# z projection spread over the value pass and the prompt attention of a one-core decoder step

## The chip, the cores and the metric

One Trainium2 chip, one core. The metric is the device time of the whole program in microseconds (us), as the median of three runs.

## What is computed

One inference step of a two-layer decoder trunk, all in float32, for a prompt of 512 positions and for 8 sequences of 4 new positions each that have 2048 past positions in a paged cache. Width 2048, 8 heads, two query/key halves of 128 per head, values of 256 per head.

```python
# layer 1: short gated convolution
b_gate, c_gate, hx, z = jnp.split(rms_norm(x, norm_g) @ w_in, 4, axis=-1)
x = x + (b_gate * conv3_causal(c_gate * hx) * silu(z)) @ w_out
# shared keys and values
k, v = jnp.split(rms_norm(x, norm_kv) @ w_kv, [QK_DIM], axis=-1)      # k: norm, rotary
# layer 2: differential attention
q, z = jnp.split(rms_norm(x, norm_g) @ w_in, [QK_DIM], axis=-1)        # q: norm, rotary
w = softmax(q1 k1 * scale) - lam * softmax(q2 k2 * scale)              # per head, masked
x = x + (rms_norm(w @ v, subln_g) * (1 - lam_init) * silu(z)) @ w_out
```

The keys and values of the past (two times 134 MB) are gathered page by page through a page table of 8 times 16 pages of 128 positions.

## The kernel before, in words

Six stages follow each other, each a block of its own with a barrier behind it: read the inputs, the convolution layer's input projection, its output projection, `project_and_score`, `attention`, `project_out`. The change touches the fourth and the fifth. Activations are held with the features on the partitions; 544 columns stand for 512 prompt positions and 32 new ones. A float32 projection is made of three products of fp32r parts (high times high, low times high, high times low), so a block of 128 output columns takes 96 matmuls of 272 columns (L1032 and L1040 in the fourth stage). Its weights are loaded in pairs of blocks (2 MB, `load_pair`), scaled by the norm gain on ScalarE (L834), copied to the high part by ScalarE (`split_hi`, L848), and the low part is the difference, made by VectorE (`split_lo`, L947).

**The fourth stage, `project_and_score`**, has 64 steps, one block each: 16 of q, 16 of z, 16 of k, 16 of v. VectorE evacuates block n-1 in step n and finishes block n-2: q and k are normed and rotated (L979 to L986), z becomes a SiLU gate with a reciprocal of 3.55 us (L971 to L974). q, k and z of the prompt go to scratch in DRAM; k and v are also turned on TensorE and written out as rows. Between this work lies the **key pass**: scores of the new positions against the past keys, cut into 128 units. A unit turns a quarter of a page's columns for four pages on VectorE (`turn_unit`, L996, four 32x32 block transposes of 128x512) and multiplies them with the queries on TensorE (`score`, L1081, 16 float32 matmuls, which are 32 records). Two units, an even and an odd one, share the four pages. A constant says how many units lie in each step, and their letters A to D say where in the step VectorE and TensorE do them. In VectorE's step n the order is: evacuate(n-1), A, finish(n-2), split_lo(n+1), B, C, D.

Half pages of keys (512 KB) arrive in a ring of six. The load of page n waits until the odd unit has turned page n-6:

```python
sp.wait_ge(kt_ready, (2 * (before // GRP) + 1) * GRP + before % GRP + 1)
```

**The fifth stage, `attention`**, begins with the softmax of the first sequence and then has 8 slots. Slot r is the value product of sequence r over its 16 pages (L1533, pages of 1 MB in a ring of eight) and, between the pages, the prompt attention of head r in four query blocks, with the softmax of sequence r+1 in five steps on VectorE. TensorE's order in a slot is written out: prompt scores of block 0, then pages 0 to 15 with turns, scores and sums behind given pages, the product with the prompt's values behind page 13 (L1504), the new values, and the sum of squares of the head's output (L1512). ScalarE issues the loads of the next head's q, k and v at the start of the next slot, when the previous head's output is done (`load_inner`), and of its z when the previous gate is done (`load_gate`). GpSimd multiplies the head's output by its norm and by the gate and writes it to scratch.

The prediction follows the lines named here, and L958 and L956 (evacuations), L1048 (sum of squares of a block), L1285 (copy of turned prompt weights), L1430 (copy of a head's output), L1489 (prompt scores).

## Time and profile before

| | |
|---|---|
| median of 3 runs | 2751.94 us (2750.53 to 2756.54) |
| profiled execution, its own time | 2754.07 us |
| its span, first to last instruction | 2752.3 us |
| TensorE / VectorE / ScalarE / GpSimd busy | 2481.1 / 1494.2 / 1017.1 / 346.9 us |
| mean granted TensorE clock | 0.956 of 2.4 GHz |
| moved by DMA | 512.01 MB, mean 186 GB/s |
| fourth stage, first to last matmul of its blocks | 1033 to 2057 us of the span |
| fifth stage, first to last value matmul | 2091 to 2506 us of the span |

Busy time is the union of an engine's instructions; a matmul's duration is its latency, several overlap, so the distance of two starts in the timeline is what an instruction costs TensorE. The granted clock is a share of 2.4 GHz; 0.5 is its lower level, 1.2 GHz.

### The profile page before, as it was taken

The page shows a single profiled execution, that of the slowest core. Times are in us where ns is not written, and L with a number is a line of the kernel's source. Part 1 is how long each engine was busy: PE and PEld are TensorE (multiplying, and loading weights), DVE is VectorE, ACT ScalarE, POOL GpSimd, SP SyncE. Part 2 cuts the span into 40 slices and gives each one's busy share as a digit, 9 for nine tenths or more (in the row PEclk, how much of TensorE's full clock was granted, in tenths as well). Part 3 has the DMA queues.
Part 4 walks back from the last instruction along what each step waited for, and adds up shares of the span by engine and source line. Part 5 has one row for each costly group of instructions (what it writes and reads, how often), then busy time and mean ns, then how long its engine had stood idle before and what let it go on. Part 6 is the DMA issues. An engine that isn't in the chain of part 4 may idle for free. (4 is left out here: it accounts for less than half of the span.)

```text
span 2752.3 us, 52718 instructions
## 1 busy us (share of the span) xinstructions
PE 2481.1 (90%) x21599; PEld 2229.3 (81%) x21599; DVE 1494.2 (54%) x1926; ACT 1017.1 (37%) x1826; POOL 346.9 (13%) x142
## 2 busy tenths in 40 slices
PE   6999999999999999999999999989995556656998
PEld 5999999999999989999898999978882122213998
DVE  3565565666563343456888887766664334324221
ACT  4121111112112226776445687745541212224121
POOL 5233333233320110000000000000000110010000
PEclk9999999999999999999999999999997778877999
DMA  4323332323323323244766778778869989986343
GB/s 129 92 77 92 92 92 76 92 83 85 92 76 112 112 86 99 85 153 135 248 237 239 268 266 267 266 243 267 281 231 361 385 343 374 381 363 245 113 120 87
DMA packets 387584, 512.01 MB, mean 186 GB/s; under 512 B 12618, under 2 KB 319700, under 8 KB 370964
## 3 DMA queue, kind: packets, MB, share of 16 engines
q1 hardware_dynamic: 328436, 449.67, 48.1%
q10 hardware_dynamic: 57792, 55.74, 5.8%
q0 software_dynamic: 1200, 4.46, 0.4%
q8 instruction: 106, 1.74, 0.3%
...
## 5 line engine op out<-in xcount | busy, mean ns | idle before, releaser
L1032 PE MATMUL psum<-x_hi,w_hi 128*128 128x272 f32 x2048 | 434.2, 293 | 3.0 <-PEq L503 3.0
L106 PE MATMUL psum<-x_hi,w_hi 128*128 128x272 f32 x2048 | 427.0, 289 | 8.4 <-DVEq L413 8.4
L106 PE MATMUL psum<-x_lo,w_hi 128*128 128x272 f32 x2048 | 426.2, 289 | 0.0
L1032 PE MATMUL psum<-x_lo,w_hi 128*128 128x272 f32 x2048 | 426.0, 289 | 0.0
L996 DVE STREAM_TRANSPOSE h_keys_turned<-h_ring 128x512 f32<-128x512 f32 x512 | 325.1, 682 | 144.3 <-DMA h_ring<-in_cache_k_dram 140.6
L1032 PEld LDWEIGHTS psum<-x_hi,w_hi 128*128 128x128 f32 x2048 | 321.7, 190 | 18.8 <-issue 18.8
L106 PEld LDWEIGHTS psum<-x_hi,w_hi 128*128 128x128 f32 x2048 | 321.5, 189 | 9.5 <-ACTq L405 9.1
L1032 PEld LDWEIGHTS psum<-x_lo,w_hi 128*128 128x128 f32 x2048 | 322.4, 189 | 0.0
L106 PEld LDWEIGHTS psum<-x_lo,w_hi 128*128 128x128 f32 x2048 | 320.9, 188 | 0.0
L366 POOL TENSOR_TENSOR w_raw<-w_raw,params 128x2048 f32<-128x2048 f32 x63 | 245.9, 3903 | 509.6 <-DMA w_raw<-in_w_in_a_dram 502.7
L1040 PE MATMUL psum<-x_hi,w_lo 128*128 128x272 f32 x2048 | 287.1, 296 | 0.0
L1040 PEld LDWEIGHTS psum<-x_hi,w_lo 128*128 128x128 f32 x2048 | 267.0, 190 | 9.4 <-issue 5.9
L114 PE MATMUL psum<-x_hi,w_lo 128*128 128x272 f32 x2048 | 266.4, 287 | 0.0
L114 PEld LDWEIGHTS psum<-x_hi,w_lo 128*128 128x128 f32 x2048 | 260.2, 188 | 0.0
L834 ACT ACTIVATE w_raw<-w_raw,params 128x256 f32<-128x256 f32 x496 | 201.6, 495 | 103.9 <-DMA w_raw<-in_w_kv_dram 58.6
L385 ACT ACTIVATE w_hi<-w_raw 128x2048 fp32r<-128x2048 f32 x64 | 122.4, 1912 | 305.1 <-PE psum L114 280.4
L422 DVE TENSOR_TENSOR w_lo<-w_raw,w_hi 128x2048 fp32r<-128x2048 f32 x64 | 175.5, 2742 | 104.1 <-ACT w_hi L385 104.1
L947 DVE TENSOR_TENSOR w_lo<-w_raw,w_hi 128x2048 fp32r<-128x2048 f32 x63 | 143.6, 2280 | 54.6 <-ACT w_hi L848 54.6
L1081 PE MATMUL psum<-h_keys_turned,h_q_blocks 128*32 128x128 f32 x4096 | 141.2, 280 | 35.1 <-DVE h_keys_turned L996 34.9
L1489 PE MATMUL psum<-head 128*128 128x128 f32 (+3 forms) x128 | 49.3, 518 | 126.4 <-DMA head<-out_new_v_prompt_dram 125.7
L1533 PE MATMUL psum<-ring,weights 128*8 128x512 f32 x1024 | 146.0, 671 | 8.0 <-DMA ring<-in_cache_v_dram 8.0
L1081 PEld LDWEIGHTS psum<-h_keys_turned,h_q_blocks 128*32 128x32 f32 x4096 | 106.4, 111 | 55.8 <-DVE h_keys_turned L996 29.3
...
## 6 DMA issues: line engine op xcount, KB each, us to landing
h_ring<-in_cache_k_dram SPq DMA_DIRECT2D x256, 512.0 KB, 6.1
ring<-in_cache_v_dram SPq DMA_DIRECT2D x128, 1024.0 KB, 12.5
...
```

The lines of the kernel that those rows point to most:

```text
L106: pe.matmul(out[:, g, 0:GT], m.WH[s][:, k * P:(k + 1) * P], x[:, k * T + g * GT:k * T + (g + 1) * GT], start=(k == 0 and x is xh), stop=Fa ...
L114: last = pe.matmul(out[:, g, 0:GT], m.WL[s][:, k * P:(k + 1) * P], xh[:, k * T + g * GT:k * T + (g + 1) * GT], start=False, stop=(k == KT ...
L366: pool.tensor_tensor(tiles(raw[p % 2][:, :]), tiles(raw[p % 2][:, :]), m.PAR[:, GA:GA + KT].unsqueeze(2).to_broadcast([P, KT, P]), ALU.mul ...
L385: act.activation(m.WH[p % 2][:, :], raw[p % 2][:, :], ACT.Copy).then_inc(hi_ready, 1)
L422: dve.tensor_tensor(m.WL[p % 2][:, :], raw[p % 2][:, :], m.WH[p % 2][:, :].bitcast(F32), ALU.subtract).then_inc(lo_ready, 1)
L834: ins = act.activation(wk, wk, ACT.Copy, scale=m.PAR[:, gain + k:gain + k + 1])
L947: dve.tensor_tensor(columns(m.PAIR_LO, n), src, tiles(m.WH[n % 2][:, :].bitcast(F32)), ALU.subtract).then_inc(lo_ready, 1)
L996: dve.transpose(kth[u % 2][:, s * QUAD:(s + 1) * QUAD], ring[n % NRING][:, u % 2 * QUAD:(u % 2 + 1) * QUAD]).then_inc(kt_ready, 1)
L1032: pe.matmul(psum[n % 2][:, g, 0:GT], m.WH[n % 2][:, k * P:(k + 1) * P], x[:, k * T + g * GT:k * T + (g + 1) * GT], start=(k == 0 and x is ...
L1040: last = pe.matmul(psum[n % 2][:, g, 0:GT], w[:, k, :], m.XH[:, k * T + g * GT:k * T + (g + 1) * GT], start=False, stop=(k == KT - 1), ski ...
L1081: last = pe.matmul(bank[a * TURN:(a + 1) * TURN, u // 2 % 2, :, u % 2, :], qblk[half % 2][:, ch * TURN:(ch + 1) * TURN], keys[:, :, a * 4 ...
L1533: last = pe.matmul(out[c * B:c * B + 2 * NEW, :], wt[r % 2][:, weights_at(p, c):weights_at(p, c) + 2 * NEW], ring[(r * NPG + p) % NR][:, c ...
```

## The change

The z blocks leave the fourth stage, which becomes 48 steps (q, k, v). The 128 key units go to steps 17 to 47, four or five in a step, with a letter E behind D. VectorE turns two pages with one instruction and lets go of ring pages in pairs; the turned keys have three buffers where there were two; a query block has 16 columns where it had 32; the rows to be written have one buffer where there were two. The first z pair is loaded, scaled and split at the end of the fourth stage.

The fifth stage projects the 16 z blocks: blocks 0 and 1 ahead of the first slot, blocks 2r+2 and 2r+3 in slot r (0 to 6), 14 matmuls ahead of each of the pages 0 to 6 and 8 to 14. Their evacuation, gate and low part are put on VectorE, their scaling, high part and exponential on ScalarE; the gates stay in SBUF, and the z scratch and its loads go. Values come as half pages (512 KB) in a ring of seven, scores of one sequence at a time, the new values in four parts. The next head's q and k are loaded when the last prompt scores are done, its v when its last product is done.

The diff, cut to its core:

```diff
-KINDS = "qzkv"
+KINDS = "qkv"
...
-FIRST_UNIT_STEP = KT + 2
-UNITS_IN_STEP = [2, 2, 2, 3] * 4 + [3, 3, 3, 2] * 4 + [4, 3, 4, 3, 3, 4, 3] * 2
+FIRST_UNIT_STEP = KT + 1
+UNITS_IN_STEP = [2] + [4, 4, 4, 4, 5] * 6
+NKTH = 3
+QN = P // TURN * NEW
...
-    return dict(zip({2: "AC", 3: "ACD", 4: "ABCD"}[many], range(first, first + many)))
+    return dict(zip({2: "CD", 4: "ABCD", 5: "ABCDE"}[many], range(first, first + many)))
...
-    unit = 8 * half + 9
+    unit = 8 * half + 10
...
-        ring = [sb(f"ring{s}", [P, HALF]) for s in range(NRING)]
-        kth = [sb(f"keys_turned{f}", [P, GRP * QUAD]) for f in range(2)]
-        qblk = [sb(f"q_blocks{f}", [P, HALF]) for f in range(2)]
+        ring = sb("ring", [P, NRING * HALF])
+        kth = [sb(f"keys_turned{f}", [P, GRP * QUAD]) for f in range(NKTH)]
+        qblk = [sb(f"q_blocks{f}", [P, HALF // TURN * QN]) for f in range(2)]
...
-                    sp.wait_ge(kt_ready, (2 * (before // GRP) + 1) * GRP + before % GRP + 1)
+                    sp.wait_ge(kt_ready, (2 * (before // GRP) + 1) * 2 + before % GRP // 2 + 1)
...
-                    after(act, rows_out[s], rows_in_slot(n) * 32)
-                    act.activation(rows[s][:, :], m.PS[:, ROWS, :], ACT.Copy).then_inc(rows_ready, 1)
-                    act.activation(srows[s][:, :], m.PS[0:GS, SROWS, 0:G * P], ACT.Copy).then_inc(rows_ready, 1)
+                    after(act, rows_out, turns_before(n) * 32)
...
-                after(dve, unit_scored, u - 1)
-                for s in range(GRP):
-                    n = u // 2 * GRP + s
+                after(dve, unit_scored, u + 1 - NKTH)
+                for pair in range(GRP // 2):
+                    n = u // 2 * GRP + 2 * pair
                     if u % 2 == 0:
-                        dve.wait_ge(page_in[n % NRING], 16 * (n // NRING + 1))
-                    dve.transpose(kth[u % 2][:, s * QUAD:(s + 1) * QUAD],
-                                  ring[n % NRING][:, u % 2 * QUAD:(u % 2 + 1) * QUAD]).then_inc(kt_ready, 1)
-                if u % 4 == 1 and u >= 5:
+                        for x in (n, n + 1):
+                            dve.wait_ge(page_in[x % NRING], 16 * (x // NRING + 1))
+                    dve.transpose(kth[u % NKTH][:, pair * 2 * QUAD:(pair + 1) * 2 * QUAD].rearrange("p (s x) -> p s x", s=2),
+                                  ring[:, n % NRING * HALF:(n % NRING + 2) * HALF].rearrange("p (s x) -> p s x", s=2)
+                                  [:, :, u % 2 * QUAD:(u % 2 + 1) * QUAD]).then_inc(kt_ready, 1)
+                if u % 4 == 2 and u >= 6:
...
-                        last = pe.matmul(bank[a * TURN:(a + 1) * TURN, u // 2 % 2, :, u % 2, :],
-                                         qblk[half % 2][:, ch * TURN:(ch + 1) * TURN], keys[:, :, a * 4 + c, :],
+                        last = pe.matmul(bank[a * TURN:a * TURN + QN, u // 2 % 2, :, u % 2, :],
+                                         qblk[half % 2][:, ch * QN:(ch + 1) * QN], keys[:, :, a * 4 + c, :],
...
-                hi_part(n, first)
+                hi_part(n, range(5))
                 if "D" in before:
                     score(before["D"])
-                hi_part(n, second)
+                hi_part(n, range(5, 11))
+                if "E" in before:
+                    score(before["E"])
+                hi_part(n, range(11, KT))
...
-    NR = 8
+    NR = 7
...
+            w, col0, _ = head_weights(d, "z")
+            def load_pair(p):
+                after(sp, zdone, 2 * p - 2)
+                sp.sem_inc(granted, 1)
+                sp.dma_start(tiles(m.PAIR_RAW[p % 2]), w.rearrange("(k p) n -> p k n", p=P)
+                             [:, :, col0 + 2 * p * P:col0 + 2 * (p + 1) * P]).then_inc(pair_in[p % 2], 16)
...
+                for f in range(2):
+                    n = 2 * (i * NPG + p) + f
+                    if n >= NR:
+                        sp.wait_ge(v_used, (n - NR) // 2 + 1)
+                    sp.sem_inc(granted, 1)
+                    sp.dma_start(ring[:, n % NR * HALF:(n % NR + 1) * HALF], cache_v[ds(page, 1), :, f * HALF:(f + 1) * HALF]
+                                 .rearrange("o p n -> (o p) n")).then_inc(half_in[n % NR], 16)
...
+            load_pair(1)
             sp.wait_ge(ids_in, 16)
             for i in range(NSEQ):
                 for p in range(NPG):
-                    n = i * NPG + p
-                    if n >= NR:
-                        sp.wait_ge(v_used, n - NR + 1)
-                    load(cache_v, i, p, n % NR)
+                    load_values(i, p)
+                    if p == 3 and i + 2 < NZ // 2:
+                        load_pair(i + 2)
...
+            def load_probs(i):
+                after(act, wt_ready, i)
+                act.dma_start(pr[:, :], st.SCORES[i]).then_inc(probs_in, 16)
...
+            def load_qk(r):
+                after(act, prompt_scored, r * TT)
...
+            def split_hi(b):
+                if not 1 <= b < NZ:
+                    return
+                after(act, zdone, b - 1)
+                after(act, zscaled, 2 * (b // 2))
+                act.activation(tiles(m.WH[b % 2][:, :]), zcolumns(m.PAIR_RAW, b), ACT.Copy).then_inc(zhi, 1)
+            def scale_half(p, f):
+                if not 1 <= p < NZ // 2:
+                    return
+                if f == 0:
+                    act.wait_ge(pair_in[p % 2], 16 * ((p + 1) // 2))
+                wp = m.PAIR_RAW[p % 2]
+                for k in range(f * KT // 2, (f + 1) * KT // 2):
+                    wk = wp[:, k * 2 * P:(k + 1) * 2 * P]
+                    ins = act.activation(wk, wk, ACT.Copy, scale=m.PAR[:, GB + k:GB + k + 1])
+                ins.then_inc(zscaled, 1)
...
             def slot(r):
-                if r:
-                    load_inner(r)
-                load_gate(r)
+                gate_exp(2 * r + 1)
                 prompt_exps(r, 0)
                 prompt_weights(r, 0)
+                split_hi(2 * r + 3)
                 prompt_exps(r, 1)
                 prompt_weights(r, 1)
+                scale_half(r + 2, 0)
                 prompt_exps(r, 2)
                 if r + 1 < NSEQ:
                     softmax_exp(r + 1)
                 prompt_weights(r, 2)
+                gate_exp(2 * r + 2)
                 prompt_exps(r, 3)
+                if r + 1 < H:
+                    load_qk(r + 1)
                 prompt_weights(r, 3)
+                scale_half(r + 2, 1)
+                split_hi(2 * r + 4)
                 act.wait_ge(o_taken, r + 1)
+                if r + 1 < H:
+                    load_v(r + 1)
                 act.activation(pp, o, ACT.Square).then_inc(osq_ready, 1)
                 act.wait_ge(osq_sum, r + 1)
-                rsqrt(act, o_ln, r * 2, m.PS[:, PSC, :], VD, m, ro[:, :])
+                rsqrt(act, o_ln, r * 2, m.PS[:, PSC, :], VD, m, ro)
+                if r + 1 < NSEQ:
+                    group_new_weights(r + 1)
+                if r + 2 < NSEQ:
+                    load_probs(r + 2)
                 take_rows(r)
...
+            def finish(b):
+                if b >= NZ:
+                    return
+                t = ztile[b % 4]
+                dve.wait_ge(zexp, b + 1)
+                chain_z.link(dve.tensor_scalar(zr[:, :], zr[:, :], 1.0, None, ALU.add))
+                chain_z.link(dve.reciprocal(zr[:, :], zr[:, :]))
+                chain_z.link(dve.scalar_tensor_tensor(out=t[:, :], in0=t[:, :], scalar=m.GSUB[:, b % 2:b % 2 + 1],
+                                                      in1=zr[:, :], op0=ALU.mult, op1=ALU.mult))
+                dve.tensor_copy(st.ZS[:, b * NT:(b + 1) * NT].rearrange("p (g t) -> p g t", g=G),
+                                grouped(t[:, :])[:, :, GP:GT]).then_inc(zready, 1)
...
+                evacuate(2 * r + 1)
+                prompt_max(r, 0, prompt)
                 step(0)
-                prompt_max(r, 0, prompt)
                 prompt_mix(r, 0, prompt)
+                finish(2 * r + 1)
+                prompt_max(r, 1, prompt)
                 step(1)
-                prompt_max(r, 1, prompt)
                 if r:
                     take_out(r - 1)
                 prompt_mix(r, 1, prompt)
+                split_lo(2 * r + 3)
                 step(2)
                 prompt_max(r, 2, prompt)
                 prompt_mix(r, 2, prompt)
+                evacuate(2 * r + 2)
                 prompt_max(r, 3, prompt)
                 step(3)
+                finish(2 * r + 2)
                 prompt_mix(r, 3, prompt)
+                split_lo(2 * r + 4)
                 step(4)
...
+            soft_max(0, first_soft)
+            split_lo(1)
+            soft_diag(0, first_soft)
+            evacuate(0)
+            soft_shift(0, first_soft)
+            soft_den(0, first_soft)
+            soft_weights(0, first_soft)
+            finish(0)
+            split_lo(2)
...
+            def project(b, part):
+                for at in range(part[0], part[1]):
+                    if at == 0:
+                        after(pe, zhi, b)
+                        after(pe, zevac, b)
+                    if at == 64:
+                        after(pe, zlo, b)
+                    if at < 64:
+                        k, x, g = at // 4, (m.XH, m.XL)[at // 2 % 2], at % 2
+                        w = m.WH[b % 2][:, k * P:(k + 1) * P]
+                    else:
+                        k, x, g = (at - 64) // 2, m.XH, at % 2
+                        w = zcolumns(m.PAIR_LO, b)[:, k, :]
+                    last = pe.matmul(zout[:, g, 0:GT], w, x[:, k * T + g * GT:k * T + (g + 1) * GT], start=(at < 2),
+                                     stop=(at >= 94), skip_group_check=True)
+                if part[1] == 96:
+                    last.then_inc(zdone, 1)
...
+            def project_in(r, p):
+                if 2 * r + 2 < NZ and p % 8 < 7:
+                    b, at = 2 * r + 2 + p // 8, p % 8 * 14
+                    project(b, (at, min(at + 14, 96)))
             def slot(r):
                 nxt = r + 1 < NSEQ
-                out = m.PS[:, OUT[r % 2], :]
+                out = m.PS[:, OUT, :]
                 prompt_scores(r, 0)
                 pe.wait_ge(wt_ready, r + 1)
-                after(pe, osb_ready, r - 1)
                 for p in range(NPG):
+                    project_in(r, p)
+                    if p == 0:
+                        after(pe, osb_ready, r)
                     value_in(pe, r, p)
...
             score_new()
-            pe.wait_ge(dve_tail, 1)
+            project(0, (0, 64))
             pe.wait_ge(new_masked, 1)
             turn_max(0)
+            project(0, (64, 96))
             spread_max(0)
+            project(1, (0, 32))
             sum_probs(0)
+            project(1, (32, 96))
+            pe.wait_ge(dve_tail, 1)
```

## Rows read from the trace of the kernel before

**Rows 1.** Busy time by stretch: window, length, engines with counts, granted clock, DMA share, GB/s.
```profile
1520.00:1765.00 245.00, 243.04 (x2797) 226.25 (x2795) 198.61 (x298) 188.21 (x385) 0.00 (x0) 1.00 0.79 263
...
1765.00:2060.00 295.00, 273.79 (x3378) 253.16 (x3370) 192.91 (x274) 147.61 (x374) 0.00 (x0) 0.98 0.78 262
...
2091.00:2507.00 416.00, 272.55 (x1533) 92.16 (x1533) 155.50 (x358) 96.62 (x218) 37.95 (x21) 0.81 0.91 368
```

**Rows 2.** Groups by form, whole span: high part of a block, z gate's reciprocal.
```profile
L848 ACT ACTIVATE w_hi<-w_raw 128x2048 fp32r<-128x2048 f32 x63 | 119.9, 1904 | 49.9 <-PE psum L1040 49.4
...
L972 DVE RECIPROCAL h_r<-h_r 128x544 f32<-128x544 f32 x16 | 56.8, 3553 | 0.6
```

**Rows 3.** TensorE in order of time, one k step: start, length, instructions, idle before.
```profile
1697.37 0.52 PE L1032 MATMUL psum<-x_hi,w_hi 128*128 128x272 f32 x2
...
1706.79 1.08 PE L1081 MATMUL psum<-h_keys_turned,h_q_blocks 128*32 128x128 f32 x32
...
1707.80 1.19 PE L1048 MATMUL psum<-h_r,ones 128*128 128x272 f32 x4
...
1714.61 0.52 PE L1032 MATMUL psum<-x_hi,w_hi 128*128 128x272 f32 x2
```

**Rows 4.** VectorE in order of time, the same k step.
```profile
1704.38 0.74 DVE L979 SCALAR_TENSOR_TENSOR h_tile<-h_plain,params,h_r 128x544 f32<-128x544 f32 x1
...
1708.43 2.28 DVE L947 TENSOR_TENSOR w_lo<-w_raw,w_hi 128x2048 fp32r<-128x2048 f32 x1
...
1710.63 2.48 DVE L996 STREAM_TRANSPOSE h_keys_turned<-h_ring 128x512 f32<-128x512 f32 x4
...
1718.05 0.71 DVE L996 STREAM_TRANSPOSE h_keys_turned<-h_ring 128x512 f32<-128x512 f32 x1 [0.95 <-DMA h_ring<-in_cache_k_dram]
```

**Rows 5.** Turns of keys (L996) alone: window, length, VectorE busy and count.
```profile
1810.00:2060.00 250.00, 122.21 (x192) 0.99 0.81 271
```

**Rows 6.** VectorE groups from 1765 to 2060 us.
```profile
L996 DVE STREAM_TRANSPOSE h_keys_turned<-h_ring 128x512 f32<-128x512 f32 x214 | 136.2, 683 | 80.7 <-DMA h_ring<-in_cache_k_dram 77.3 <-PE psum L1081 3.2
...
L956 DVE TENSOR_TENSOR h_tile<-psum,rs 128x544 f32<-128x544 f32 x16 | 11.1, 695 | 15.3 <-DMA k_scratch<-h_tile 12.8 <-PE psum L1040 2.6
```

**Rows 7.** VectorE evacuates block 17, in order of time.
```profile
1273.78 0.72 DVE L958 TENSOR_TENSOR h_plain<-psum,rs 128x544 f32<-128x544 f32 x1 [2.29 <-PE psum L1040]
```

**Rows 8.** TensorE from the last blocks to the first value page.
```profile
2057.44 1.95 PE L1081 MATMUL psum<-h_keys_turned,h_q_blocks 128*32 128x128 f32 x64
...
2066.76 1.08 PE L1062 MATMUL psum<-ident,h_tile 128*128 128x128 f32 x4 [6.56 <-ACT h_srows L860]
...
2073.24 1.89 PE L1463 MATMUL psum<-q_sample,k_sample 128*32 128x32 f32 x32 [4.97 <-PEq L1756]
...
2090.91 5.10 PE L1533 MATMUL psum<-ring,weights 128*8 128x512 f32 x24
```

**Rows 9.** TensorE in slot 2, and its last value pages.
```profile
2210.34 1.19 PE L1489 MATMUL psum<-head 128*128 128x128 f32 x4 [15.09 <-DMA head<-out_new_v_prompt_dram]
...
2240.74 1.90 PE L1533 MATMUL psum<-ring,weights 128*8 128x512 f32 x16
...
2243.43 1.98 PE L1512 MATMUL psum<-head,ones 128*128 128x512 f32 x4
...
2504.17 1.90 PE L1533 MATMUL psum<-ring,weights 128*8 128x512 f32 x16
```

**Rows 10.** ScalarE scales a pair of blocks, in order of time.
```profile
1714.89 6.51 ACT L834 ACTIVATE w_raw<-w_raw,params 128x256 f32<-128x256 f32 x16 [3.19 <-DMA w_raw<-in_w_kv_dram]
```

**Rows 11.** ScalarE in slot 2: exponentials of query block 2.
```profile
2224.91 0.58 ACT L1280 ACTIVATE head<-psum,prompt_max 128x384 f32<-128x384 f32 x1
```

**Rows 12.** VectorE in slot 2: end of its mix, start and end of the softmax weights.
```profile
2226.89 0.62 DVE L1393 SCALAR_TENSOR_TENSOR head<-head,prompt_inv 128x384 f32<-128x384 f32 x1
...
2233.41 0.55 DVE L1360 RECIPROCAL inv_denom<-psum 128x64 f32<-128x64 f32 x1
...
2235.84 0.67 DVE L1370 TENSOR_TENSOR weights<-probs 128x512 f32<-128x512 f32 x1
```

307 lines of the change are left out of this document (166 added, 141 removed).

## Prediction

> **What bounds the kernel now.** I read the busy time by stretch first. TensorE is busy 243.0 of 245 us while k blocks and keys run together, 273.8 of 295 us with v blocks and keys, but only 272.6 of 416 us in the value pass, at a granted clock of 0.81 [rows 1]. The reader is to see one engine with holes in one stage alone. There the DMA share is 0.91. So the change has something to fill: 16 blocks of projection are taken out of a stage that TensorE fills and put into one that it doesn't. The question is what bounds the shorter fourth stage once TensorE no longer does, and how much of the value pass's holes survive.
>
> **Part 1, the fourth stage.** On TensorE a high part of 64 matmuls with one unit between them takes 9.42 us, from 1697.37 to 1706.79; a unit takes 1.01, so a matmul costs 0.13 us with the seams and a block of 96 about 12.1 [rows 3]. Removing 16 blocks takes 16 x 12.1 = 193 us from TensorE. A k step with three units takes 17.24 us (1697.37 to 1714.61); with 4.2 units it would take 17.24 + 1.2 x 1.1 = 18.6, a v step, without the sum of squares (0.9), 17.7. If TensorE set the pace, steps 18 to 47 (16 that finish q or k, 14 that don't) would take 16 x 18.6 + 14 x 17.7 = 545 us.
>
> I think that VectorE and the ring of key pages set it. VectorE turns a unit in four times 0.6 = 2.4 us; finishing a k block takes 4.05 (1704.38 to 1708.43), the low part 2.2 [rows 4]. With 4.2 units, evacuation and the turned scores a k step has 17.5 us of VectorE work against TensorE's 18.6, without any wait. The waits come from the ring: page n may be loaded only when page n-6 has been turned by the odd unit, and the even unit needs it six pages later. When the odd unit begins at 1710.63, its second page is done at 1711.85; the page that takes this slot is turned at 1718.05: 6.2 us [rows 4]. Before, three units in a step left other work to cover this. At 5.2 us per unit (192 turns, so 48 units, in 250 us) [rows 5] it already shows: VectorE waited 77.3 us for pages in 295 us [rows 6].
>
> In the changed code pages are let go in pairs, so the second page's load is issued one issue later: I take 6.2 + 0.6 = 6.8 us. A cycle of two units (one group of four pages) is then 6.8, plus the even unit's second half and the odd unit's first half, 1.2 each: 9.2 us. VectorE work that lies between an even and an odd unit is added to it; what lies between an odd and an even one is hidden. By the written order, four units in a step and alternating phases, exposed are: in a v step low part 2.2 and turned scores 0.6 in one phase, evacuation 0.6 and turned scores 0.6 in the other, mean 2.0, or 1.0 per group; in a k step 6.9 in the one and 2.9 in the other, 2.3 per group. For pages behind a pair of weights, which are later, I add 0.2. So 10.4 us per group in v steps and 11.7 in k steps. Units 2 to 127 are 33.5 groups in k steps and 29.5 in v steps: 33.5 x 11.7 + 29.5 x 10.4 = 392 + 307 = 699 us. The first v evacuations wait for the scratch stores as before, 12.8 us [rows 6], of which the pages that land meanwhile give back more than half: 5 us.
>
> The start: block 17 is evacuated at 1273.78 [rows 7], and step 17 now has two units too, so step 18 begins at 1275. The last block ends at 1275 + 704 = 1979 us, before at 2057.4. From there to the first product of the fifth stage it was 15.8 us (2057.44 to 2073.24) [rows 8]; with one buffer for rows the last three stores follow one another, 5 us more. The fifth stage begins at 2000, **73 us earlier**. Bounds: TensorE's pace of 545 us (another 154 earlier) and the cycle with 7.8 us of latency (63 later).
>
> The query blocks of 16 columns, three key buffers and the new places of D and E cost and give nothing here, since TensorE waits for VectorE; their range is 0 to the rival below. ScalarE keeps some 17 us of work in a k step of 24; that covers it, and if it didn't, the steps would lengthen by the difference to 24, which is none.
>
> **Part 2, the start of the fifth stage.** Before, 17.7 us lie between its first product (2073.24) and the first value page (2090.91) [rows 8]. Now 192 matmuls precede it, 24.0 us, and 2 more while the clock is low. They fill the waits of the softmax (some 10 us); then come the gate and the low part of block 2 on VectorE before block 1 is evacuated, which block 2 waits for. Walking the order I get 36.6 us: **18.9 later**. Bounds 12 and 26.
>
> **Part 3, a slot.** Slot 2 takes 33.1 us from its scores to the sum of squares (2210.34 to 2243.43) [rows 9]; 1.4 of it is a wait for VectorE and about 2 the low clock after 15.09 us without work. Both go: 29.7. Added: 192 matmuls, 24.0 + 0.3. The sum of squares and the norm up to the next scores: 2.8. Together 56.8 us. The head wait of 15 us is gone, since q and k are asked for some 20 us and v some 50 us ahead of use.
> New waits, from the written orders:
> - Block 2r+3 begins at page 8 and needs block 2r+2 evacuated. VectorE does this behind the mix of query block 2, whose exponentials stand on ScalarE behind `scale_half`: 8 instructions, half of 6.51, 3.3 us [rows 10]. That starts when the turn behind page 6 is copied. Scaling 3.3, exponentials to end of mix 2.6 (2224.91 to 2227.51) [rows 11, 12], evacuation 0.7, hand-overs 0.5: 7.1, of which one page covers 0.9. With 0.5 for the copy: **6.7**.
> - At the end `split_hi` follows the second `scale_half` (3.3 + 1.9 [rows 2]), then on VectorE the low part 2.2, softmax weights 3.1 (2233.41 to 2236.51) [rows 12] and the copy of the output; page 14 with its matmuls, page 15 and the new values cover most of it: **2.7** remain.
> - Page 0 waits for ScalarE to copy the previous rows, behind four new copies and a load: **1.0**.
> Queues: on SP the z pair stands behind page 3 of a slot and waits for block 2r+1, which is done by then; pages 4 and 5 come after its 2 MB, some 7 us of DMA, and TensorE asks for page 4 some 12 us later, so I give it 0. On GpSimd's queue four small loads of the new values take the place of one, ahead of the first slot, at 0 for they are used at its end. The scores of one sequence (0.5 MB) are asked for at the end of a slot and used at the start of the one after.
> The gates' 2 x 5.1 us of VectorE (reciprocal 3.55 [rows 2]) lie beside TensorE's matmuls; without that cover they would come in front of max or mix, 5 us each.
> A slot is 67.2 us. DMA moves 16.8 + 1.6 + 2.1 + 1.0 = 21.5 MB in it, 320 GB/s, below the 368 of [rows 1], so it isn't the bound. From first to last value page: 7 x 67.2 + 34 for slot 7, which projects nothing = 504; before 2505.9 - 2090.9 = 415 [rows 8, 9]. **89 later.** Bounds for a slot: 60 (only half of each wait and 56.8 of work) and 71.
>
> **Sum** against the profiled span of 2752.3: -73 + 19 + 89 = +35, so 2787. The profiled execution took 2754.07, 2.1 above the median of 2751.94; against the median it is 2787 again, +1.3%.
>
> Clock: after 6.56 us without work four turns took 1.08 us [rows 8], at 1.2 GHz, where the clock had been full. A wait of 6.7 us in each slot could do the same to the next 3 us of projection, 1.5 us per slot. By the Trainium skill, "TensorE: Matmul & The Clock Gate", section "Loop structure matters more than you think", idle stretches between bursts bring the lower clock back; that speaks against this change, and with it the sum would be 2797. I leave it out because the later wait for VectorE absorbs most of it.
>
> **Rivals.**
> - *The page latency is mostly hidden* (0.17). TensorE sets the pace of the fourth stage: -227 + 108 = -119, 2633. For it: TensorE was busy 243 of 245 us in the k steps [rows 1]. Against: units came at 5.2 us, not 4.2, in the v steps [rows 5]. In this case the unit's cost counts. The Trainium skill, the same page, section "LDWEIGHTS (loading the stationary operand)", has a load's time go by its columns; 16 for 32 would save up to 50 us by it and give 2585. The records that bear on it start every 0.03 us [rows 3], which doesn't tell load from product.
> - *In between* (0.23): a latency near 6 us and slots of 63. The stage takes 45 us less, the slots 30 less: 2712. The sign turns at a latency of 6.2 with my slots, or slots of 62 with my latency.
> - *My forecast, slower* (0.48), own range 2750 to 2830: the ring of six pages decides, from 10.0 us per group on.
> - *The value pass becomes worse* (0.12): half pages and a lookahead of 3.5 pages instead of eight let DMA run dry whenever TensorE is held up; slots of 72: 2821.
> That the change doesn't do what it says could be so of the early head loads: if z weights and values go ahead of them, v is late at page 13. I give it nothing of its own.
>
> **How the numbers follow.** Predicted 2787. The range of 2645 to 2832 leaves out most of the first rival and the ends. About 0.2%, 5.5 us, is what a measurement can tell from no change. Faster 0.38 (both first rivals less their upper ends, and the low end of mine), same 0.07, slower 0.55.
>
> **What would show it.** Right: L996 waits for DMA by 250 us or more; k steps of 24 and v steps of 22 us; matmuls of the fourth stage with 5 us of waits for L996 in a step; slots of 67 us with one wait of 6 to 7 us at page 8 that VectorE's evacuation ends; no wait for head loads. Wrong: steps below 20 us, or slots that DMA ends.

## The result and the profile after

The changed kernel takes 2870.62 us (median of 4 runs, 2865.84 to 2878.27) against 2753.48 for the kernel before, a ratio of **1.0428, 95% interval 1.0401 to 1.0455**. The profiled execution took 2869.0 us with a span of 2867.2, 114.9 above the 2752.3 of before. I had predicted +35: the direction is right, the time is 39 us above the upper end of the range.

Where the 80 us between +35 and +115 lie is read from TensorE's timeline at the seams of the stages. The first product of the fifth stage (L1600) starts at 2028.96, predicted 2000: 29 us. From it to the first value page (2063.97) it is 35.0, predicted 36.6. From there to the first product with the new values, which follows the last value page (L1700 at 2620.35; L1554 at 2505.89 before), it is 556.4, predicted 504: 52.4 us. The three differences make the 80. So both stages that the change touches are worse than I had them, the slots more so.

The busy time by stretch, of the changed kernel (stretch, its length, then busy us of each engine with its instructions, the granted clock, DMA share, GB/s); the first three answer to [rows 1], the fourth is slots 0 to 6, from the scores of one to the scores of the last:

```profile
1520.00:1765.00 245.00, 192.45 (x2264) 170.80 (x2263) 147.42 (x151) 127.12 (x311) 0.00 (x0) 0.90 0.72 239
1765.00:2004.00 239.00, 202.23 (x2489) 182.61 (x2488) 138.76 (x121) 103.93 (x272) 0.00 (x0) 0.92 0.76 257
2064.00:2507.00 443.00, 371.64 (x2295) 233.68 (x2294) 224.91 (x346) 142.03 (x301) 28.39 (x20) 0.89 0.81 288
...
2059.00:2571.00 512.00, 434.69 (x2701) 273.85 (x2700) 265.73 (x411) 159.89 (x341) 34.04 (x24) 0.90 0.81 286
```

The reader is to see that TensorE, which filled 243 of 245 us of the k steps before, now has 192 there and a granted clock of 0.90; and that the value pass, whose holes were to be filled, has 371.6 of 443 busy, at 0.89, with DMA at 0.81, lower than before. No engine is full in any of these stretches. What holds the kernel are waits.

Of the same profile, the costliest groups (line, engine, what it does, count, busy us and mean ns, then the idle time before them and what ended it); the first answers to L996 of the kernel before, whose line for the whole span stands below:

```profile
L979 DVE STREAM_TRANSPOSE h_keys_turned<-h_ring 128x1024 f32<-128x1024 f32 x256 | 303.0, 1219 | 272.2 <-DMA h_ring<-in_cache_k_dram 272.2
...
L1068 PE MATMUL psum<-h_keys_turned,h_q_blocks 128*16 128x128 f32 x4096 | 155.6, 299 | 141.5 <-DVE h_keys_turned L979 138.5
...
L1679 PE MATMUL psum<-ring,weights 128*8 128x512 f32 x1024 | 143.4, 641 | 30.5 <-DMA ring<-in_cache_v_dram 27.7
L1592 PE MATMUL psum<-x_hi,w_hi 128*128 128x272 f32 x512 | 123.0, 325 | 41.0 <-DVE z_tile L1421 41.0
```

The same turns in the kernel before:

```profile
L996 DVE STREAM_TRANSPOSE h_keys_turned<-h_ring 128x512 f32<-128x512 f32 x512 | 325.1, 682 | 144.3 <-DMA h_ring<-in_cache_k_dram 140.6 <-PE psum L1081 3.4
```

VectorE waits 272 us for key pages, 141 before (the 77.3 of [rows 6] are those of 295 us of the stage), and TensorE 138.5 us for turned keys behind it, 34.9 before.

**One cycle of the ring**, VectorE's timeline in two k steps (start, length, line, xcount, in brackets the idle time before it and what ended it; `x3` from 1352.55 is the second half of an even unit and both halves of an odd one):

```profile
1352.55 3.50 DVE L979 STREAM_TRANSPOSE h_keys_turned<-h_ring 128x1024 f32<-128x1024 f32 x3 [4.73 <-DMA h_ring<-in_cache_k_dram]
1355.97 0.68 DVE L948 TENSOR_TENSOR h_plain<-psum,rs 128x544 f32<-128x544 f32 x1
1356.85 1.25 DVE L979 STREAM_TRANSPOSE h_keys_turned<-h_ring 128x1024 f32<-128x1024 f32 x1 [0.19 <-DMA h_ring<-in_cache_k_dram]
1362.11 1.25 DVE L979 STREAM_TRANSPOSE h_keys_turned<-h_ring 128x1024 f32<-128x1024 f32 x1 [4.02 <-DMA h_ring<-in_cache_k_dram]
...
1370.14 3.49 DVE L979 STREAM_TRANSPOSE h_keys_turned<-h_ring 128x1024 f32<-128x1024 f32 x3
1377.94 3.50 DVE L979 STREAM_TRANSPOSE h_keys_turned<-h_ring 128x1024 f32<-128x1024 f32 x3 [4.30 <-DMA h_ring<-in_cache_k_dram]
1381.36 0.69 DVE L948 TENSOR_TENSOR h_plain<-psum,rs 128x544 f32<-128x544 f32 x1
```

The odd unit's first half ends at 1354.85 and lets two pages go; the even unit that needs their successors goes on at 1362.11, 7.3 us later. I worked this out for all 63 groups of four pages after the first: in 59 of them VectorE waited there, and the pages came on average **7.6 us** after the turn that freed their places (6.2 to 11.3, the long ones behind a pair of weights). The second load of a pair, the one that VectorE waits for, goes out on average 1.9 us after that turn, 1.15 us behind the first of the pair, and lands 5.6 us after its issue. The evacuations at 1355.97 and 1381.36 make a k step of 25.4 us; the mean is 26.3 us for the k steps 18 to 33 and 22.7 us for the v steps 34 to 47.

**A slot**, TensorE's timeline (waits of over 0.7 us in slot 3, one value page without a wait, and the start of slot 4):

```profile
2282.01 1.22 PE L1626 MATMUL psum<-head 128*128 128x128 f32 x4 [0.78 <-ACT prompt_weights L122]
2302.95 1.82 PE L1679 MATMUL psum<-ring,weights 128*8 128x512 f32 x8 [3.26 <-DMA ring<-in_cache_v_dram]
...
2307.79 1.04 PE L1679 MATMUL psum<-ring,weights 128*8 128x512 f32 x8
...
2320.03 0.79 PE L1592 MATMUL psum<-x_hi,w_hi 128*128 128x272 f32 x2 [5.89 <-DVE z_tile L1421]
2353.43 2.97 PE L1650 MATMUL psum<-prompt_probs,ones 128*128 128x512 f32 x4 [2.43 <-ACT prompt_probs L1378]
2357.17 1.22 PE L1626 MATMUL psum<-head 128*128 128x128 f32 x4 [0.78 <-ACT prompt_weights L122]
```

The scores of the slots start at 2059.0, 2130.8, 2206.2, 2282.0, 2357.2, 2431.3, 2507.0 and 2570.8: a slot takes **75.3 us** from slot 1 to slot 5, predicted 67.2. Slot 6, for which no further z pair is loaded or scaled, takes 63.8. Behind each of the three long waits the matmuls take longer: eight with a value page 1.82 us where they take 1.04 without a wait, the first pair of the projection 0.79 where it takes 0.49 in the run with scaling later, the sums of squares 2.97 where they take 1.98 there. The wait at page 8 comes from ScalarE, as predicted:

```profile
2313.20 0.38 ACT L1319 ACTIVATE prompt_weights<-psum 128x256 f32<-128x256 f32 x1 [12.23 <-PE psum L1634]
2313.49 3.29 ACT L1345 ACTIVATE w_raw<-w_raw,params 128x256 f32<-128x256 f32 x8
2316.67 0.56 ACT L1312 ACTIVATE prompt_probs<-psum,prompt_max 128x384 f32<-128x384 f32 x1
```

What ends page 4 is in SP's queue: the load of the z pair (L1212) goes out 6 us into the slot, and the pages issued behind it are those for which TensorE waits until 2302.95. The pair lands 12.3 us after its issue, the two halves of page 4 13.6 and 14.9 us after it, and TensorE is ready for them 11.7 us after it. In slots 1 to 5 the pair takes 11.1 to 12.6 us and the second half of page 4 is there 13.9 to 15.2 us after the pair's issue, TensorE after 11.7 each time.

```profile
2274.42 13.44 SPq L1222 DMA_DIRECT2D ring<-in_cache_v_dram  x5
2287.97 0.39 SPq L1212 DMA_DIRECT2D w_raw<-in_w_in_b_dram  x1
2289.53 9.89 SPq L1222 DMA_DIRECT2D ring<-in_cache_v_dram  x7
```

### The profile page after: what moved, and what is told of

Read it like the earlier page. It is cut to its first block and busy times, and to the rows that moved or that the text cites. A ratio compares the mean times of both kernels' runs of the same rounds, so it can differ in the third digit from the quotient of the medians.

```text
span 2867.2 us, 53321 instructions
## 1 busy us (share of the span) xinstructions
PE 2553.8 (89%) x21599; PEld 2281.3 (80%) x21599; DVE 1488.0 (52%) x1671; ACT 1021.6 (36%) x1858; POOL 351.0 (12%) x152
## 5 line engine op out<-in xcount | busy, mean ns | idle before, releaser
L979 DVE STREAM_TRANSPOSE h_keys_turned<-h_ring 128x1024 f32<-128x1024 f32 x256 | 303.0, 1219 | 272.2 <-DMA h_ring<-in_cache_k_dram 272.2
L106 PE MATMUL psum<-x_hi,w_hi 128*128 128x272 f32 x2048 | 427.0, 289 | 8.4 <-DVEq L413 8.4
L106 PE MATMUL psum<-x_lo,w_hi 128*128 128x272 f32 x2048 | 426.0, 289 | 0.0
L1017 PE MATMUL psum<-x_hi,w_hi 128*128 128x272 f32 x1536 | 332.9, 298 | 3.0 <-PEq L503 3.0
L1017 PE MATMUL psum<-x_lo,w_hi 128*128 128x272 f32 x1536 | 324.6, 293 | 0.0
L106 PEld LDWEIGHTS psum<-x_lo,w_hi 128*128 128x128 f32 x2048 | 320.8, 188 | 0.0
L1068 PE MATMUL psum<-h_keys_turned,h_q_blocks 128*16 128x128 f32 x4096 | 155.6, 299 | 141.5 <-DVE h_keys_turned L979 138.5
L114 PE MATMUL psum<-x_hi,w_lo 128*128 128x272 f32 x2048 | 266.4, 287 | 0.0
L114 PEld LDWEIGHTS psum<-x_hi,w_lo 128*128 128x128 f32 x2048 | 260.1, 188 | 0.0
L1017 PEld LDWEIGHTS psum<-x_lo,w_hi 128*128 128x128 f32 x1536 | 246.9, 193 | 0.0
L1068 PEld LDWEIGHTS psum<-h_keys_turned,h_q_blocks 128*16 128x16 f32 x4096 | 110.9, 103 | 169.1 <-DVE h_keys_turned L979 90.0
L1025 PE MATMUL psum<-x_hi,w_lo 128*128 128x272 f32 x1536 | 227.9, 305 | 0.0
L422 DVE TENSOR_TENSOR w_lo<-w_raw,w_hi 128x2048 fp32r<-128x2048 f32 x64 | 173.0, 2703 | 104.2 <-ACT w_hi L385 104.2
L1025 PEld LDWEIGHTS psum<-x_hi,w_lo 128*128 128x128 f32 x1536 | 211.8, 200 | 7.4 <-issue 3.2
L830 ACT ACTIVATE w_raw<-w_raw,params 128x256 f32<-128x256 f32 x384 | 155.9, 494 | 98.3 <-DMA w_raw<-in_w_kv_dram 73.7
L1592 PE MATMUL psum<-x_hi,w_hi 128*128 128x272 f32 x512 | 123.0, 325 | 41.0 <-DVE z_tile L1421 41.0
## 6 DMA issues: line engine op xcount, KB each, us to landing
w_raw<-in_w_kv_dram SPq DMA_DIRECT2D x16, 2048.0 KB, 12.4
```

What stands on the lines that cost most here:

```text
L106: pe.matmul(out[:, g, 0:GT], m.WH[s][:, k * P:(k + 1) * P], x[:, k * T + g * GT:k * T + (g + 1) * GT], start=(k == 0 and x is xh), stop=Fa ...
L114: last = pe.matmul(out[:, g, 0:GT], m.WL[s][:, k * P:(k + 1) * P], xh[:, k * T + g * GT:k * T + (g + 1) * GT], start=False, stop=(k == KT ...
L422: dve.tensor_tensor(m.WL[p % 2][:, :], raw[p % 2][:, :], m.WH[p % 2][:, :].bitcast(F32), ALU.subtract).then_inc(lo_ready, 1)
L830: ins = act.activation(wk, wk, ACT.Copy, scale=m.PAR[:, gain + k:gain + k + 1])
L979: dve.transpose(kth[u % NKTH][:, pair * 2 * QUAD:(pair + 1) * 2 * QUAD].rearrange("p (s x) -> p s x", s=2), ring[:, n % NRING * HALF:(n % ...
L1017: pe.matmul(psum[n % 2][:, g, 0:GT], m.WH[n % 2][:, k * P:(k + 1) * P], x[:, k * T + g * GT:k * T + (g + 1) * GT], start=(k == 0 and x is ...
```

## The experiments

Theory: in the fourth stage the latency of a key page, on a ring of six, sets the pace; in the slots three waits, each of order and not of bandwidth, and the low clock behind them. Rivals: VectorE's written order holds TensorE in the fourth stage; DMA sets the slot.

### The fourth stage

**No key loads.** Only the first six pages are loaded; the scores are those of these pages.

```diff
                 if n >= NRING:
-                    before = n - NRING
-                    sp.wait_ge(kt_ready, ...)
+                    return
...
                         for x in (n, n + 1):
-                            dve.wait_ge(page_in[x % NRING], 16 * (x // NRING + 1))
+                            if x < NRING:
+                                dve.wait_ge(page_in[x], 16)
```

> The changed kernel with only the first six key pages loaded; all later turns work on the pages that are there, so no load of keys and no wait for one is left (the scores are those of six pages only). Theory (the ring's latency paces the fourth stage: 272 us of L979 waiting for pages, 734 us from step 17 to the end of block 47): TensorE's own work paces it, 545 us plus what VectorE's order adds, so the stage ends 150 to 190 us earlier and the whole takes 2680 to 2720 us; the granted clock of the stage is back near 1. Rival (VectorE's written order holds TensorE, and the page waits only fill time in which it would have been held anyway): the stage gets less than 60 us shorter, the whole stays above 2810 us. A TensorE wait for L979 of over 60 us would speak for the rival.

Measured: 2725.8 us in one run, 6 above the range of the theory and far below the rival's; the fifth stage begins at 1887.1, 142 us earlier, where the theory had 150 to 190. TensorE still waits 29.5 us for turned keys, which no page delays: so much of the stage is VectorE's order, and it is under the 60 us that would have spoken for the rival. From step 18 to the end of block 47 it takes 595 us where the changed kernel takes 729. The v steps take 17.2 us, with TensorE busy for 239 of 240 us; the k steps take 22.2 us, at a granted clock of 0.95, and all but 1 us of these waits lie there.

```profile
L979 DVE STREAM_TRANSPOSE h_keys_turned<-h_ring 128x1024 f32<-128x1024 f32 x256 | 297.6, 1212 | 18.3 <-PE psum L1068 18.1
...
L1068 PE MATMUL psum<-h_keys_turned,h_q_blocks 128*16 128x128 f32 x4096 | 139.6, 278 | 32.1 <-DVE h_keys_turned L979 29.5
```

**Pages let go one by one.**

```diff
-                for pair in range(GRP // 2):
-                    n = u // 2 * GRP + 2 * pair
+                for s in range(GRP):
+                    n = u // 2 * GRP + s
...
-    sp.wait_ge(kt_ready, (2 * (before // GRP) + 1) * 2 + before % GRP // 2 + 1)
+    sp.wait_ge(kt_ready, (2 * (before // GRP) + 1) * GRP + before % GRP + 1)
```

> The changed kernel, but each key page is turned and let go by itself, as in the kernel before (four turns of 0.6 us in a unit, not two of 1.2). In the changed kernel the page that VectorE waits for lands on average 7.6 us after the turn that frees its buffer, where I had taken 6.8. Theory (the two loads of a pair are issued together and share the DMA engines, which makes the later one late): latency falls to 6.2 to 6.8 us, some 0.9 us in each of 63 groups, 40 to 60 us less in the stage, the whole 2810 to 2835 us. Rival (the latency is that of one load, whoever lets it go, and of the weights in the queue): under 15 us of difference, 2855 to 2875 us.

Measured: 2824.6 us in one run, 46 less. Worked out as above from the timeline, the latency is now 6.4 us on average (112 waited pages), 1.2 less than in pairs. A load goes out 1.1 us after the turn that frees its place, where the second of a pair did after 1.9, and lands 5.2 us later, where that one took 5.6. So two thirds of the 1.2 are the second issue and one third is a slower landing; that the two loads of a pair share the DMA engines, as the theory has it, isn't shown, and could explain the landing alone. The gain came to the size that the theory gave. The waits of its turns:

```profile
L978 DVE STREAM_TRANSPOSE h_keys_turned<-h_ring 128x512 f32<-128x512 f32 x512 | 324.5, 682 | 200.0 <-DMA h_ring<-in_cache_k_dram 199.9
```

**Ring of eight.**

```diff
-NRING = 6
+NRING = 8
-NKTH = 3
+NKTH = 2
```

> The changed kernel with eight key pages in the ring in place of six, and two buffers of turned keys in place of three, which frees the room. A page is then asked for when the group before the last is turned, a whole group earlier. Theory (latency of the ring): a group of four pages takes about 8.8 us in place of 11.6, as TensorE's work sets it; the fourth stage ends 130 to 180 us earlier, the whole takes 2690 to 2740 us, below the kernel before. L979 waits for pages under 80 us. Rival (two buffers of turned keys are too few, or VectorE's order holds TensorE): the gain is under 60 us, the whole stays above 2810 us, and VectorE waits for units scored instead.

Measured: **2738.9 us (6 runs), ratio to the kernel before 0.9945, interval 0.9928 to 0.9962**: 132 us less than the changed kernel, and now 0.5% below the kernel before. The fifth stage begins at 1900.0, in place of 2029.0. Waits for pages fall from 272 to 62 us with a latency that is no shorter (median landing 6.6 us, 5.8 before); it is covered, since each page is asked for a group earlier.

```profile
L979 DVE STREAM_TRANSPOSE h_keys_turned<-h_ring 128x1024 f32<-128x1024 f32 x256 | 301.5, 1219 | 84.2 <-DMA h_ring<-in_cache_k_dram 62.0 <-PE psum L1068 21.9
...
h_ring<-in_cache_k_dram SPq DMA_DIRECT2D x256, 512.0 KB, 6.6
```

The rival falls: the order is unchanged, and there is one buffer of turned keys less. What it named is there, but small: VectorE now waits 21.9 us for TensorE's scores (L1068), as there are two buffers of turned keys, and TensorE 40.0 us for turned keys.

### The slots

**Scaling later**, alone on the changed kernel.

```diff
-                scale_half(r + 2, 0)
                 prompt_exps(r, 2)
                 if r + 1 < NSEQ:
                     softmax_exp(r + 1)
+                scale_half(r + 2, 0)
```

> The changed kernel, with the first half of the z pair's scaling (8 instructions, 3.3 us on ScalarE) moved behind the exponentials of query block 2 and of the sequence's softmax. Theory (this order delays the exponentials, the mix and the evacuation that block 2r+3 waits for, 5.89 us at page 8 in slots 0 to 5, and the clock is low after it): the wait falls below 2.8 us (what slot 6, without scaling, shows) and each of six slots gets 4 to 5 us shorter, the whole 25 to 30 us, 2840 to 2846 us. Rival (the DMA queue sets the slot, and time saved at page 8 comes back as waits for value pages): the slots stay at 75 us within 1 us, the whole 2864 to 2872 us, and waits for the ring grow by what page 8 loses.

Measured: 2849.9 us (ratio to before 1.0352, 1.0324 to 1.0380), 21 less. The slots 1 to 5 take 71.4 us, 3.8 less, of which the wait is 3.2 (5.89 to 2.71). Over seven slots it is 23 us; the fourth stage of this run ended 1.9 us later. That is short of the 25 to 30, at the size of 4 us per slot. The wait at page 4 grew by 0.2 us on average, so the time wasn't given back. The wait of 2.43 us at the sum of squares is unchanged, but in slots 0 to 2 the lower clock no longer follows it (1.98 us for four matmuls, 2.4 to 3.0 in the changed kernel); in slots 3 to 5 it does. So the length of a wait alone doesn't say whether it costs the clock. Slot 2's wait at page 8 and at its sum of squares:

```profile
2235.79 0.49 PE L1592 MATMUL psum<-x_hi,w_hi 128*128 128x272 f32 x2 [2.72 <-DVE z_tile L1421]
2269.17 1.98 PE L1650 MATMUL psum<-prompt_probs,ones 128*128 128x512 f32 x4 [2.43 <-ACT prompt_probs L1378]
```

**No value loads.** Only the first seven half pages are loaded; the attention over cached values is that of these.

```diff
                     if n >= NR:
-                        sp.wait_ge(v_used, (n - NR) // 2 + 1)
+                        return
...
-                eng.wait_ge(half_in[n % NR], 16 * (n // NR + 1))
+                if n < NR:
+                    eng.wait_ge(half_in[n % NR], 16 * (n // NR + 1))
```

> The changed kernel with only the first seven half pages of values loaded; all later pages use what is there, so that the only large load left in a slot is the z pair (the attention over the cached values is that of these half pages only). In the changed kernel a slot with a z pair takes 75.3 us from scores to scores, slot 6, which loads and scales no pair, 63.8, and slot 7, which projects nothing, some 50 where I had predicted 34. Theory (DMA ends page 4 in slots 1 to 5 by some 3.2 us each and sets slot 7): without the loads slots 1 to 5 lose 3 to 5 us each, slot 7 takes 33 to 37 us, the whole 2825 to 2840 us. Rival (the slot is set by the chain over ScalarE and VectorE, and the wait at page 4 only takes the place of another one): slots stay above 74 us and only slot 7 gets shorter, 2850 to 2858 us.

Measured: 2825.8 us in one run, 45 less. Slots 1 to 5 take 69.9 us, 5.4 less, and slot 7, from its scores to the last turn of rows, 40.2 in place of 55.7, which is above the 33 to 37 expected; from its first value page to the new values it takes 30.7 in place of 46.2. So DMA has 5 us in a slot and 15 in the last. The 69.9 us that remain are the slot's work, the two waits of order (5.89 and 2.43 us, both still there) and the low clock behind them.

**Ring of eight and a new order in the slot.**

```diff
                 if r + 1 < NSEQ:
                     softmax_exp(r + 1)
+                scale_half(r + 2, 0)
...
                     load_qk(r + 1)
+                scale_half(r + 2, 1)
                 prompt_weights(r, 3)
-                scale_half(r + 2, 1)
...
                 prompt_max(r, 2, prompt)
+                evacuate(2 * r + 2)
                 prompt_mix(r, 2, prompt)
-                evacuate(2 * r + 2)
```

> The ring of eight key pages, and in a slot: both halves of the z pair's scaling placed behind the exponentials of query blocks 2 and 3, and block 2r+2 evacuated before the mix of query block 2. Theory (each of the three waits in a slot is one of order, 5.9 us at page 8, 2.4 at the sum of squares, and the low clock after them): page 8 waits under 1 us, the sum of squares under 0.5, slots 0 to 5 take 66 to 69 us; with the ring's 2739 this gives 2680 to 2700 us. Rival (DMA sets the slot once TensorE is faster): the slots stay at 70 us or more, with ring waits of 5 us or more at page 4, 2705 to 2720 us.

Measured: 2668.2 us (0.9694, 0.9679 to 0.9708), 71 less than with the ring alone, where 39 to 59 were expected. The waits at page 8 and at the sum of squares are gone, a slot takes 64.4 us. The wait at page 4 is what is left, 2.8 to 4.1 us:

```profile
2118.45 0.71 PE L1626 MATMUL psum<-head 128*128 128x128 f32 x4 [0.78 <-ACT prompt_weights L122]
2138.78 1.89 PE L1679 MATMUL psum<-ring,weights 128*8 128x512 f32 x8 [3.53 <-DMA ring<-in_cache_v_dram]
2183.13 0.71 PE L1626 MATMUL psum<-head 128*128 128x128 f32 x4 [0.78 <-ACT prompt_weights L122]
```

**And the z pair in quarters** (behind value pages 2, 4, 6 and 8, with a semaphore for each half).

```diff
-                    if p == 3 and i + 2 < NZ // 2:
-                        load_pair(i + 2)
+                    if p in (2, 4, 6, 8) and i + 2 < NZ // 2:
+                        load_quarter(i + 2, p // 2 - 1)
```

> As the kernel with a ring of eight and the new order in the slot, with the z pair's load of 2 MB cut into four of 0.5 MB, put behind value pages 2, 4, 6 and 8 in the queue. Theory (the value pages behind the pair are late by its 2 MB, and the ring of 3.5 pages can't cover this): the wait at page 4, 3 us or more in slots 1 to 5, falls below 1 us, 15 to 25 us in all, 2660 to 2680 us. Rival (DMA bandwidth as a whole, not the order in the queue, sets it): the same waits in smaller pieces, under 5 us of difference to the run without quarters.

Measured: **2639.5 us (0.9593, 0.9579 to 0.9608)**, 29 less, where 15 to 25 were expected, and a slot of 59.2 us. The wait at page 4 is gone, and with it the lower clock behind it (1.89 us for eight matmuls in the lines above). The same bytes are moved in less time, at a DMA share of 0.95: it was the place of the pair in the queue, not the bandwidth. The pieces are smaller and most of them go out later; which of the two does how much, no run shows. The stretch of slots 0 to 6 (columns as above):

```profile
1926.00:2340.00 414.00, 398.22 (x2701) 248.05 (x2699) 251.73 (x411) 158.42 (x340) 33.78 (x24) 1.00 0.95 354
```

It has the 2701 matmuls of the 512 us in the changed kernel. Of the 98 us between them 36.5 are busy time (434.7 to 398.2), at a granted clock of 0.90 and of 1.00, and 61.5 are idle time.

**The mended slots with the ring of six** (order and quarters, `NRING = 6`, `NKTH = 3`).

> The changed kernel with the new order in the slot and the z pair in quarters, but with its own fourth stage: six key pages, let go in pairs, three buffers of turned keys. Theory (the two stages add up: the ring cost 132 us, order and quarters 100 us): 2765 to 2780 us, at or above the kernel before, so that the ring alone decides the sign. Rival (the gains overlap, for instance through the clock): outside 2755 to 2790 us.

Measured: 2773.7 us in one run. The two parts add up (2639.5 + 132), and without the ring's two pages even the mended slots don't make the change pay.

**Pages one by one in the ring of eight** (the edit of the single pages on top of the quarters).

> The kernel with ring of eight, new order and quarters (2639 us), and the key pages turned and let go one by one. Theory (with eight pages each is asked for a group earlier, so its latency of 6.4 or 7.6 us is covered either way; 40 us of TensorE waits for turned keys remain, at the two ends and behind weight pairs): 2628 to 2643 us. Rival (latency still paces a part of the stage): 2600 to 2625 us.

Measured: 2640.8 us (0.9592, 0.9576 to 0.9608), no difference. With each page asked for a group earlier, it costs nothing whether pages are let go in pairs or one by one; with the ring of six it cost 46 us.

### Parts of the change on the kernel before

**Early head loads.**

```diff
-                if r:
-                    load_inner(r)
                 load_gate(r)
...
                 prompt_exps(r, 3)
+                if r + 1 < H:
+                    after(act, prompt_scored, (r + 1) * TT)
+                    load_head(r + 1, 0)
+                    load_head(r + 1, 1)
                 prompt_weights(r, 3)
                 act.wait_ge(o_taken, r + 1)
+                if r + 1 < H:
+                    load_head(r + 1, 3)
```

> The kernel before with one part of the change alone: q and k of the next head are loaded behind the last scores of this one, v behind the last product with v, not all at the start of the slot; and TensorE waits for v at page 13 only. In the kernel before each of slots 1 to 7 begins with a wait for these loads, 15.09 us in slot 2. Theory (in that kernel the value pass is bound by DMA, share 0.91, 19.4 MB in a slot of 53 us, so the wait is time in which the ring fills up and is given back later): 0 to 25 us faster, and TensorE waits for value pages instead. Rival (the wait is on the path): 7 slots by 8 to 15 us, 55 to 100 us faster, 2650 to 2700 us.

Measured: 2704.2 us (0.9822, 0.9809 to 0.9836), 48 less: neither range. The value pass of the kernel before waits 123.7 us for heads in seven slots; 39% of that came out as time. Then DMA is full, at a slot of 46 us, and TensorE waits 42.3 us for pages in place of 8.0. The value pass, of the kernel before and of this one:

```profile
2091.00:2460.00 369.00, 241.97 (x1350) 81.66 (x1349) 143.34 (x325) 88.30 (x195) 32.53 (x18) 0.82 0.92 376
```

```profile
2091.00:2460.00 369.00, 284.97 (x1540) 92.77 (x1540) 157.85 (x365) 96.63 (x218) 38.15 (x21) 0.90 1.00 414
```

I had taken a share of 0.91 for full.

**Query blocks of 16 columns.**

```diff
-                        last = pe.matmul(bank[a * TURN:(a + 1) * TURN, u // 2 % 2, :, u % 2, :],
-                                         qblk[half % 2][:, ch * TURN:(ch + 1) * TURN], ...
+                        last = pe.matmul(bank[a * TURN:a * TURN + QN, u // 2 % 2, :, u % 2, :],
+                                         qblk[half % 2][:, ch * QN:(ch + 1) * QN], ...
```

> The kernel before with one part of the change alone: query blocks of 16 columns in place of 32 in the scores of the keys (4096 weight loads and matmuls in the fourth stage), with the banks blanked once. In the kernel before TensorE is busy 243 of 245 us of the k steps, so what a unit saves there is seen. Theory (a weight load of 16 columns takes as long as one of 32, in the traces 103 and 111 ns: no gain): within 0.2% of the kernel before. Rival (the load's time goes by its columns, as the Trainium skill's page on TensorE's matmul has it, in the section on the load of the stationary operand): 20 to 50 us faster, units of 0.7 us in place of 1.01.

Measured: 0.9992, interval 0.9981 to 1.0002 (12 runs). The weight loads of the fourth stage, 1270 to 2057 us, in the kernel before and in this one:

```profile
L1081 PEld LDWEIGHTS psum<-h_keys_turned,h_q_blocks 128*32 128x32 f32 x4032 | 104.7, 111 | 55.7 <-DVE h_keys_turned L996 29.3 <-issue 14.0
```

```profile
L1086 PEld LDWEIGHTS psum<-h_keys_turned,h_q_blocks 128*16 128x16 f32 x4032 | 100.9, 97 | 54.8 <-DVE h_keys_turned L998 27.5 <-issue 20.4
```

A unit of 32 records takes 1.07 us with 16 columns and 1.08 with 32 [rows 3]. The Trainium skill, "TensorE: Matmul & The Clock Gate", section "LDWEIGHTS (loading the stationary operand)", gives a load half the time for half the columns; here it went from 111 to 97 ns and none of it reached the time, so the measurement decides.

**The best that the study found with z left in place:** early heads, query blocks of 16, a ring of eight (the rotation's buffer shared with `r` makes room).

> The kernel before, its z blocks where they were, with what the study found that fits it: early loads of the heads (2704 us by themselves), query blocks of 16 columns, and a ring of eight key pages, for which the narrower blocks and one buffer less make room. Theory (moving z is worth something by itself, since this kernel's slots are set by DMA, share 1.00, with TensorE at 285 of 369 us, while the fourth stage is set by TensorE): the ring gives back at most the 35 us that TensorE waits for turned keys in the v steps, 2670 to 2695 us, and the kernel with z moved, ring of eight, new order and quarters stays 30 us or more faster. Rival (the move only shifts work between two stages that are full): 2645 us or less.

Measured: 2672.5 us (0.9707, 0.9691 to 0.9722). The fourth stage's k steps and its value pass (columns as above):

```profile
1270.00:1760.00 490.00, 489.04 (x5561) 458.37 (x5559) 422.45 (x560) 316.46 (x675) 0.00 (x0) 1.00 0.76 258
...
2091.00:2420.00 329.00, 249.46 (x1379) 82.39 (x1380) 137.15 (x321) 87.44 (x195) 38.11 (x21) 0.93 1.01 422
```

Here each stage is full on one engine: TensorE in the one, DMA in the other. The kernel with z moved and both parts mended is 33 us faster (2639.5). The two also differ in their value pages (halves or whole), the order of a slot and the units of a step, so the 33 us are the difference of the best kernels of either kind in this study, not a price of the move alone.

## Why the prediction was right or wrong

The sign was right, and so was its main reason. The time lay above the range because three terms were too small: the latency of the ring, the wait at page 4, which was put at nothing, and the low clock, which was left out.

- **The ring sets the fourth stage, not TensorE.** Right, and what tipped the sign. VectorE's waits for pages by 250 us or more: 272. Without loads the stage takes 595 us in place of 729 from step 18 to the end of block 47, where I had 545 for TensorE's pace. That bound was right in the v steps (17.2 us for 17.7) and too low in the k steps (22.2 for 18.6), where VectorE's order makes TensorE wait 28.5 us and the granted clock is 0.95.
- **"I take 6.2 + 0.6 = 6.8 us."** The first step that failed, by size: with the 0.2 for pages behind weights I had 7.0, and it is 7.6. I charged letting go in pairs with one issue of 0.6 us; 1.15 us lie between the two issues of a pair, and single pages show 6.4. The rest of the cycle was right: from the even unit's second half to the odd unit's first it takes 4.7 us in k steps and 3.4 in v steps, which are my 2.4 of turns with 2.3 and 1.0 of other work. A group takes 12.4 and 11.0 us (11.7 and 10.4), over 63 groups 38 us more. Of these 25 reached the last block: block 47 ends at 2004, predicted 1979, because I had put its end 5 us behind the turns, and it lies 7 us before the last one. The upper bound of 7.8 held the latency. k steps take 26.3 us (24), v steps 22.7 (22).
- **The end of the stage** took 25 us where I had 21, near by luck. The 5 us for stores one after another aren't there: from the last scores to the fifth stage it is 14.7 us, 13.9 before. In their place are 4.4 and 0.9 us of waits for the last keys, and the 32 matmuls of either of the last two units take 1.91 us where they take 1.07 at the full clock.
- **The start of the fifth stage**, 36.6 us: 35.0. Right.
- **The wait at page 8**, 6.7 us behind `scale_half`: 5.9 in slots 0 to 5, at the place and for the reason given, and 2.7 in slot 6, which scales nothing. **Sum of squares**, 2.7: 2.4. Right. **Page 0**, 1.0: none of that size.
- **"pages 4 and 5 come after its 2 MB, some 7 us of DMA, and TensorE asks for page 4 some 12 us later, so I give it 0."** The second step that failed. TensorE asks 11.7 us later, as said, but the pair takes some 12 us and not 7, and the second half of page 4 lands after 13.9 to 15.2. A ring of 3.5 pages doesn't reach over this: 3.2 us in slots 1 to 5, some 16 us; quarters took 29 out of the time, with the clock. By bytes it is right that DMA isn't the bound (share 0.81), but an average of a stretch can't see this.
- **"I leave it out because the later wait for VectorE absorbs most of it."** The third, and the largest. The clock costs 36.5 us of busy time in slots 0 to 6, over 5 us per slot, where I had put 1.5 in a sentence beside the sum. The clock falls behind three waits in a slot, not one, and I had counted with one. By the Trainium skill's rule in "TensorE: Matmul & The Clock Gate", section "Loop structure matters more than you think", long waits between matmuls bring the lower clock back, and this trace agrees: 0.90 with the waits, 1.00 without.
- **The slots in sum:** 512 us for slots 0 to 6 where I had 470. The clock's 36.5 us and the 17 us of waits for value pages make 12 more than this, so by difference the waits of order came out some 12 us below my forecast.
- **Slot 7 at 34 us**: 46.2 from its first value page, and 30.7 without value loads. Half pages leave 3.5 pages ahead, and DMA then sets the slot. It is my fourth rival's mechanism, in one slot.
- **My first rival, 2633 us**, is where the mended kernel ends (2639.5), and that is luck in part. Its mechanism, TensorE sets the pace once the latency is covered, was sound, and its condition wasn't met by a ring of six. But it had the fifth stage begin 227 us earlier than before and the value pass take 89 us longer; in the mended kernel it begins 177 us earlier (1896.2) and the value pass takes 43 us longer, with slots of 59.2 and not 67.2 us. The two errors cancel.
- The **work of a slot, 56.8 us**, is confirmed by the 59.2 of the mended kernel, of which 0.8 + 0.9 + 0.4 are waits.
- **Query blocks and the third key buffer at nothing**: the blocks shown, on the kernel before, where TensorE is full; the buffer only in so far as the kernel with two of them is not held by it. The **head wait** is gone, as said, but in the kernel before only 39% of it was on the path.
